# Last feed-forward of a two-block transformer: eight of its eleven up groups by 26 block products instead of 28, the weights' row and column sums on VectorE

## The reference, cut to what matters

```python
def swiglu(y, w_in, w_out):
    a, b = jnp.split(y @ w_in, 2, axis=-1)
    return (jax.nn.silu(a) * b) @ w_out

x = ada_out(x, swiglu(ada_in(x, mod, 2, norm_pre[l, 2]), ffn_w_in[l, 1], ffn_w_out[l, 1]),
            mod, 2, norm_post[l, 2], 0.5)
```

## Time and profile before

| what | value |
|---|---|
| median of 3 runs | 2141.54 us (2141.37 to 2142.06) |
| span of the profiled execution | 2137.4 us |
| TensorE busy | 2103.9 us, 98% of the span |
| VectorE busy | 1093.4 us, 51% |
| GpSimd busy | 721.6 us, 34% |
| ScalarE busy | 514.0 us, 24% |
| TensorE clock granted, mean | 0.997 |

### The profile page before, as it was taken

One profiled execution on the slowest core, in us unless ns is written; L12 is line 12 of the kernel. 1 busy time (PEld: TensorE's weight loads), 2 busy tenths in 40 slices (PEclk: granted clock), 3 DMA queues, 4 the chain that ended last, 5 costly groups with the idle time before them and its releaser, 6 DMA issues. The chain is left out here.

```text
span 2137.4 us, 25867 instructions
## 1 busy us (share of the span) xinstructions
PE 2103.9 (98%) x9961; PEld 1695.4 (79%) x9961; DVE 1093.4 (51%) x2049; ACT 514.0 (24%) x1240; POOL 721.6 (34%) x571
## 2 busy tenths in 40 slices
PE   7999999999999999999999999999999999999998
PEld 4446777777788888888888888888556888888887
DVE  7987956655443873445435534543726341122444
ACT  3443433334440000101400111113234330110101
POOL 0100200000105666654365665630011125456642
PEclk9999999999999999999999999999999999999999
DMA  9752455454222455234135533331222222222231
GB/s 379 238 186 87 137 198 185 141 157 129 81 79 80 158 173 169 55 82 125 48 119 180 174 106 82 82 106 50 77 86 94 65 79 79 79 96 78 75 88 40
DMA packets 244492, 252.27 MB, mean 118 GB/s; under 512 B 9946, under 2 KB 194708, under 8 KB 244116
## 3 DMA queue, kind: packets, MB, share of 16 engines
q1 hardware_dynamic: 243488, 249.17, 36.7%
q10 hardware_dynamic: 884, 1.46, 0.3%
HBM read 245.12 MB, written 4.21 MB: 117 GB/s over the span
## 5 line engine op out<-in xcount | busy, mean ns | idle before, releaser
L2428 POOL TENSOR_TENSOR w_sums<-ring 128x512 f32<-128x512 f32 x66 | 89.3, 1354 | 368.1 <-POOLq L1628 288.3
L2456 POOL TENSOR_TENSOR hidden<-rstd,h_act 128x256 f32<-128x256 f32 x66 | 53.8, 816 | 336.2 <-DVE h_act L2645 336.2
L2645 DVE TENSOR_TENSOR h_act<-ps,rstd 128x256 f32<-128x256 f32 x78 | 33.1, 424 | 221.1 <-PE ps L2328 124.6
L2310 PE MATMUL ps<-h_sums,w_sums 128*128 128x256 f32 x528 | 126.5, 380 | 0.8 <-DVE h_sums L2580 0.4
L2322 PE MATMUL ps<-h_sums,w_sums 128*128 128x256 f32 x528 | 125.0, 379 | 2.0 <-DVE rstd L2614 2.0
L2267 PE MATMUL ps<-h_act,ring 128*128 128x256 f32 x528 | 125.2, 381 | 1.2 <-ACT h_act L1995 1.2
L2333 PE MATMUL ps<-h_act,w_sums 128*128 128x256 f32 x528 | 124.8, 379 | 0.0
L2316 PE MATMUL ps<-h_act,ring 128*128 128x256 f32 x528 | 124.7, 379 | 0.0
L2328 PE MATMUL ps<-h_sums,ring 128*128 128x256 f32 x528 | 124.7, 379 | 0.0
L2275 PE MATMUL ps<-h_act,ring 128*128 128x256 f32 x528 | 124.4, 379 | 0.0
L2614 DVE TENSOR_TENSOR rstd<-ps,h_act 128x256 f32<-128x256 f32 x72 | 30.6, 425 | 164.6 <-PE ps L2310 142.9
(11 more groups left out here) (498 smaller groups left out, 4305.7 us busy)
## 6 DMA issues: line engine op xcount, KB each, us to landing
ring<-in_ffn_w_in SPq DMA_DIRECT2D x66, 1024.0 KB, 7.6
ring<-in_w_mod SPq DMA_DIRECT2D x12, 2048.0 KB, 7.9
ring<-in_w_gate_up SPq DMA_DIRECT2D x22, 1024.0 KB, 7.8
ring<-in_ffn_w_out SPq DMA_DIRECT2D x32, 704.0 KB, 5.7
mod_half<-in_w_ada SPq DMA_DIRECT2D x16, 1024.0 KB, 8.9
ring<-in_w_in SPq DMA_DIRECT2D x7, 2048.0 KB, 10.2
ring<-in_ffn_w_out SPq DMA_DIRECT2D x8, 1408.0 KB, 7.0
ring<-in_w_down SPq DMA_DIRECT2D x16, 704.0 KB, 5.8
```

What stands on the lines that cost most here:

```text
L2310: last = pe.matmul(pb, s2[:, k], F.t2[:, k], start=(k == 0), stop=(k == 3))
L2428: pool.tensor_tensor(s1, a21, a22, ALU.add).then_inc(S["wsum"].sem, 1)
L2456: pool.tensor_tensor(one[:, j], F.gate1[f % 2], F.got21[f % 2], ALU.mult)
L2645: dve.tensor_tensor(out21, pc, F.v, ALU.add).then_inc(S["got21"].sem, 1)
```

## The change

Units 0 to 3 (groups 0 and 1) and units 20 and 21 (group 10) stay as they are. Groups 2 to 9 are each computed as one product of 4x4x2 blocks: the weights' 1024 rows in four blocks of 256, the 512 columns in four blocks of 128, the tokens in two halves. The plain way has 32 block products; this one 26, each of two `matmul` calls, so 52 calls a group. `PAIR_UNITS[2]` names the groups; calls 0 and 1 have none and keep their instructions.

Before the pair groups VectorE forms the token arguments once (`pair_args`: 30 sums of 128x512, both sources in SBUF, drawn by the `spare(2)` of units 0 to 2). For each group TensorE does three rounds of four products with unchanged weights, three rounds of two products with weight differences, four with the row sums and four with the column sums of the weights. GpSimd forms the six differences (128x256 each) and multiplies the hidden values in 128x512 pieces; ScalarE copies 5 pieces out of PSUM and does two silus of 128x512; VectorE forms the rest, and the two sums of the weights, each one `tensor_reduce` over all 4096 elements of a partition. The diff, cut to its core (`F.units` for `UNITS`, `F.ups` for `FT` and the renaming of `f` to `u` are left out):

```diff
+PAIR_UNITS = {0: (), 1: (), 2: tuple(range(2, 10))}
+ROUNDS = (((1, 0), (3, 2)), ((0, 2), (1, 3)), ((0, 3), (1, 2)))
...
+def pair_tensor(K, F, pe, e):
...
+    products(0)
+    if e:
+        R["f"].wait(pe, 3 * e)
+    products(1)
+    R["begun"].wait(pe, 2 * e + 1)
+    differences(0)
...
+        R["full"].wait(pe, e)
+    products(2)
+    R["f"].wait(pe, 3 * e + 1)
+    differences(1)
+    R["w"].wait(pe, 3 * e + 1)
+    R["rows"].wait(pe, e + 1)
+    for i in range(4):
+        last = product(F.round_banks(e, 0)[i // 2], i % 2, F.rows[:, :, i], F.x_val[i], True, i % 2 == 0)
+    last.then_inc(R["d1"].sem, 1)
+    R["f"].wait(pe, 3 * e + 2)
+    differences(2)
+    R["w"].wait(pe, 3 * e + 2)
+    R["cols"].wait(pe, e + 1)
+    for i in range(4):
+        last = product(F.round_banks(e, 1)[i // 2], i % 2, F.cols[:, 2 * i:2 * i + 2], F.block(i, 1), True, i % 2 == 0)
+    last.then_inc(R["d2"].sem, 1)
...
+def pair_rows(K, F, dve, e):
...
+    dve.tensor_reduce(F.rows.rearrange("p k i n -> p (k i n)"), w.rearrange("p (q m) -> p m q", q=4), AX.X,
+                      ALU.add).then_inc(R["rows"].sem, 1)
...
+def pair_vector(K, F, dve, e):
...
+    R["begun"].wait(dve, 2 * e + 2)
+    R["s"].wait(dve, 3 * e + 1)
+    dve.tensor_tensor(w[:, 0:4:3], halves(F.round_banks(e, 0)[0]), total[:, 0:3:2], ALU.subtract).then_inc(R["w"].sem, 1)
+    for r in (1, 2):
...
+        R["y_kept"].wait(dve, 2 * e + r)
+        dve.tensor_tensor(total[:, 0:2], total[:, 0:2], halves(one), ALU.subtract)
+        dve.tensor_tensor(total[:, 2:4], total[:, 2:4], halves(two), ALU.add).then_inc(R["f"].sem, 1)
+    pair_columns(K, F, dve, e)
+    R["s"].wait(dve, 3 * e + 2)
+    dve.scalar_tensor_tensor(w[:, 1:3], halves(F.round_banks(e, 1)[0]), 0.5, yk[0], ALU.mult,
+                             ALU.subtract).then_inc(R["w"].sem, 1)
+    R["w"].wait(dve, 3 * e + 2)
+    dve.tensor_tensor(c[:, 1:3], w[:, 0:2], w[:, 2:4], ALU.add)
+    dve.tensor_tensor(c[:, 0:4:3], w[:, 1:3], w[:, 0:4:3], ALU.subtract).then_inc(R["c"].sem, 1)
+    if last:
+        t2, t1, t4, t3 = F.token_sums(LEAD)
+        dve.tensor_tensor(t3, F.h22, F.h12, ALU.subtract).then_inc(R["token"].sem, 1)
+        R["token"].wait(dve, 1)
+        dve.tensor_tensor(t2, t3, F.h11, ALU.add).then_inc(R["token"].sem, 1)
+    R["d1"].wait(dve, e + 1)
+    R["f"].wait(dve, 3 * e + 2)
+    for i, bank in enumerate(F.round_banks(e, 0)):
+        ins = dve.tensor_tensor(total[:, 2 * i:2 * i + 2], total[:, 2 * i:2 * i + 2], halves(bank), ALU.add)
+    ins.then_inc(R["f"].sem, 1)
+    R["s"].wait(dve, 3 * e + 3)
+    R["c"].wait(dve, 2 * e + 1)
+    dve.tensor_tensor(w[:, 0:2], halves(F.round_banks(e, 2)[0]), yk[1], ALU.subtract).then_inc(R["w"].sem, 1)
...
+    if last:
+        dve.tensor_tensor(t4, F.h21, t2, ALU.subtract).then_inc(R["token"].sem, 1)
+    else:
+        pair_rows(K, F, dve, e + 1)
...
+def pair_differences(K, F, pool, e, r):
...
+        R["s"].wait(pool, 3 * e - 2 + r)
...
+def pair_columns(K, F, dve, e):
...
+    dve.tensor_reduce(F.cols, w.rearrange("p (k i n) -> p k n i", k=KT, i=4), AX.X, ALU.add).then_inc(R["cols"].sem, 1)
...
@@ fast_tensor
+    for u, f in enumerate(F.tiles):
+        if u == LEAD:
+            for e in range(len(F.pairs)):
+                pair_tensor(K, F, pe, e)
...
+            if F.pairs:
+                F.rows_kept.wait(pe, len(ROWS_AT))
+                F.R["w"].wait(pe, 3 * len(F.pairs))
@@ fast_vector
+    if F.pairs:
+        steps = pair_args(K, F, dve)
...
+        if F.pairs and u == LEAD:
+            F.R["hid"].wait(dve, len(F.pairs))
...
+        if F.pairs and LEAD <= u < F.ups:
+            if u > LEAD:
+                S["hid"].wait(dve, u)
+            a, b = (0, 9) if u == LEAD else (9, FH - 1)
+            dve.tensor_tensor(xs[:, a:b], b12[:, a:b], b11[:, a:b], ALU.add).then_inc(S["xsum"].sem, b - a)
@@ kernel
-    nc = bacc.Bacc("TRN2", target_bir_lowering=False, num_devices=1)
+    nc = bacc.Bacc("TRN2", target_bir_lowering=False, num_devices=1, dynamic_dma_scratch_size=1024)
```

More of the change, by code:

```diff
@@ L2196, in fast_fields @@
     F.call, F.prev, F.W, F.context = call, prev, W, context
-    F.S = {n: Tally(K.fast[n], K.fast_base[n]) for n in FAST_COUNTS}
-    for n, count in FAST_COUNTS.items():
+    F.S = {n: Tally(K.fast[n], K.fast_base[n]) for n in FAST_SEMS}
+    F.pairs = PAIR_UNITS[call]
+    F.tiles = [f for f in range(FT) if f // 2 not in F.pairs]
+    F.ups = len(F.tiles)
+    F.units = F.ups + 4
+    for n, count in fast_counts(F.ups).items():
         K.fast_base[n] += count
@@ new lines, in pair_hidden, with pair_weights, product, products @@
+def pair_hidden(F, e, half):
+    f = 2 * F.pairs[e]
+    tiles = F.W.hid[:, :, :, :].rearrange("p a f n -> p (a f) n")
+    a, b = (2 * FH * (f // FH) + FH * half + f % FH for f in (f, f + 1))
+    return tiles[:, a:b + 1:b - a, :]
+def pair_weights(w):
+    return w.rearrange("p (k i n) -> p k i n", k=KT, i=4)
+def pair_tensor(K, F, pe, e):
+    R, S = F.R, F.S
+    w = pair_weights(K.ring.take(pe, ("up", F.call, F.pairs[e])))
+    def product(bank, at, weights, tokens, first, begins):
+        for k in range(2):
+            last = pe.matmul(bank[:, HALF * at:HALF * at + HALF], weights[:, k], tokens[:, k], start=(begins and k == 0),
+                             stop=(k == 1), skip_group_check=True)
+        return last
+    def products(r):
+        one, two = F.round_banks(e, r)
+        for at, (i, j) in enumerate(ROUNDS[r]):
+            R["args"].wait(pe, 2 * r + at + 1)
+            product(one, at, w[:, 2 * j:2 * j + 2, i], F.x_arg[i, j], True, at == 0)
+        for at, (i, j) in enumerate(ROUNDS[r][::-1] if r == 2 else ROUNDS[r]):
+            last = product(two, at, w[:, 2 * i:2 * i + 2, j], F.y_arg[i, j], True, at == 0)
+        last.then_inc(R["t"].sem, 1)
+    def differences(r):
+        one = F.round_banks(e, r)[0]
+        R["diff"].wait(pe, 3 * e + r + 1)
+        for at, (i, j) in enumerate(ROUNDS[r]):
+            last = product(one, at, F.diff[:, r, at], F.s_arg[i, j], False, False)
+        last.then_inc(R["s"].sem, 1)
+    if e == 0:
+        S["got21"].wait(pe, LEAD - 1)
+        S["got12"].wait(pe, LEAD - 1)
+    else:
+        R["w"].wait(pe, 3 * e)
+    products(0)
[4 more added lines that the diff above has]
+    differences(0)
+    if e == 0:
+        S["got21"].wait(pe, LEAD)
+        S["got12"].wait(pe, LEAD)
+    else:
+        R["full"].wait(pe, e)
[14 more added lines that the diff above has]
+    last.then_inc(R["d2"].sem, 1)
+    K.ring.left(R["d2"].sem, R["d2"].base + e + 1)
@@ L2323, in fast_tensor @@
         last.then_inc(S["p5"].sem, 1)
-        if f >= LEAD - 1:
-            sum_11(f)
-        S["w"].wait(pe, f + 1)
+        if u >= LEAD - 1:
+            sum_11(u)
+        S["w"].wait(pe, u + 1)
+        if F.pairs and u == LEAD:
+            F.R["token"].wait(pe, 4)
         for k in range(4):
-            last = pe.matmul(pc, a22[:, k], F.t4[:, k], start=False, stop=(k == 3), skip_group_check=True)
+            last = pe.matmul(pc, a22[:, k], t4[:, k], start=False, stop=(k == 3), skip_group_check=True)
@@ L2560, in fast_scalar @@
         x_square(K, T, act, 0)
[L2561 removed]
+    S["got12"].wait(act, F.units)
     y_square(K, T, act, 9, K.h[:, 3, CTX + HALF:TOK])
```

431 lines of the change are left out of this document (321 added, 110 removed).

## The result

The changed kernel takes 2180.39 us (median of 4 runs, 2179.04 to 2180.70) against 2141.45 us before: 1.0183 times the time, 95% interval 1.0171 to 1.0196. The prediction was 2168 us, range 2139 to 2198. So the sign and the range held, and the number was 12 us short.

A forecast was written before the change was run, and what follows sets the result against it. TensorE bounds the kernel before; in the pair groups its loop through w3 and VectorE's own work were to meet at 26.0 us. Pair groups +14.7, arguments +8.4 and leaving the pairs +3.5 gave +26.6 us: 2168 us, range 2139 to 2198.

The forecast's parts named there:

- Price of the reductions: In `pair_rows` and `pair_columns`, each VectorE reduction over 4096 elements takes 7.4 us, the middle between 4.4 and 10.5.
- the upper end: 10.5 us for each reduction, at 2.54 ns an element, from the hopping write of L1154.
- VectorE's other work: VectorE's operations in a pair group beside the two reductions take 11.0 us, waits included.
- The cycle: Pair group: TensorE's loop through w2 and w3 and VectorE's own work both 25.8 us; 26.0 a group, +14.7 for eight.
- t3: The end of `products(2)` of a pair group, taken as time zero; unhindered, the next comes 22.45 us later.
- Two signs: In the pair groups: TensorE idle before `products(0)`, released by VectorE; VectorE's share in the steady stretch near 100%.
- dear reductions: Rival, pair groups: reductions cost nearer to the hopping write, R = 10.5 us; 2180 to 2216 us, 2195 its number; chance 0.22.
- Arguments: Units 0 to 2: VectorE's 30 argument sums put 8.4 us on the path, p5 waiting for v; from nothing to 11.
- Leaving the pairs: Last group and unit 20: p1 waits 2.4 us for w3, p5 another 1.1 to 1.8; together 3.5, from 2 to 5.
- GpSimd, ScalarE, SyncE at nothing: Pair groups: GpSimd some 8 us of 26, ScalarE below 5, SyncE's loads unchanged; none adds time.
- The contiguous reductions: Rival, pair groups: reductions run at the in-order price, R = 4.4 us; 23.6 a group, 2149 us (2138 to 2158); chance 0.30.
- The faster case: Rival: contiguous reductions, hidden arguments (`spare` pair below 1.39 us), no contention at the c sums; 2136 us; chance 0.10.

## Why the prediction was right or wrong

- **Price of the reductions: right, by luck.** 7.4 us was taken as the middle between in order and a hopping write; 7.35 and 7.23 were measured, and in order 4.4, the lower end. But the write that gave the upper end was not slow by its hop alone. GpSimd was busy beside it, and VectorE's sums just ahead of it, which hop nowhere, took 1.21 us for the usual 0.69 (kernel before, VectorE, then GpSimd):

```profile
77.08 1.21 DVE L1148 TENSOR_TENSOR raw_t<-raw_t,cst 128x512 f32<-128x512 f32 x1
78.21 1.21 DVE L1150 TENSOR_TENSOR tmp<-tmp,cst 128x512 f32<-128x512 f32 x1
79.45 1.46 DVE L1154 TENSOR_TENSOR kv_t<-raw_t,tmp 128x512 f32<-128x512 f32 x1
...
75.66 9.13 POOL L1119 TENSOR_TENSOR h_act<-x_res,ctx_rstd 128x256 f32<-128x256 f32 x8 [24.33 <-ACT ctx_rstd L1100]
```

  Against these neighbours the hopping write costs 0.25 us more, not 0.77. By that the upper end would have been 6.2 us and the middle 5.3 (estimates); how the hop and GpSimd's work add up no run shows. So that the write agrees with a page's price for small hops says little. The Trainium skill's 1.73 ns an element (Vector Engine (DVE) Microarchitecture Reference, section 5.2) is close to the 1.77 and 1.79 measured; its remark on a single stream that alternates between two regions at full rate doesn't carry over to these two reads.
- **VectorE's other work: right.** The PSUM sums take 0.68 to 0.69 us, the 256-wide ones 0.42; a steady group's eighteen instructions beside the reductions keep VectorE busy for 10.4 us, where 11.0 were forecast with the waits.
- **The cycle: right as far as it went.** w2 10.4 us behind t3 was the forecast; 1822.39 + 10.08 = 1832.47 is where the column products start. 26.0 us a group were forecast, 25.8 are measured where the clock stays up. Two signs did not come. The gap ahead of `products(0)` is none: by the forecast's own numbers the column products end at 10.4 + 3.45 = 13.9, behind w3 at 13.6. And VectorE was busy for 24.95 of the second group's 27.41 us, 91% and not near 100%: the loop through w2 sets the pace, not VectorE's total, as the run with the rows in order shows.
- **The step that failed** is in "The cycle of a pair group": TensorE's products behind a wait were priced at 0.432 us a call, the price of an engine that never idles. Behind the waits they ran at half clock, which cost 16.5 us in the groups and 1.75 in unit 20. This term was missing, and it alone is more than the 12 us by which the forecast was short. The loop itself, at full clock, is 25.6 us (10.08 + 3.45 + 12.09) and not 26.0, which takes 3 us off again. That the time still lies in the range is luck: its upper part stood for dear reductions, and these were not dear. The forecast named the wait of 3 us and did not ask what it does to the clock. The Trainium skill has the rule (TensorE: Matmul & The Clock Gate, "Part 1: The HAM clock gate"): the array's clock falls to 1.2 GHz behind idle time. The granted clock of 0.50 behind the gap agrees.
- **Arguments: right in size.** 8.4 us forecast, 7.6 measured, with waits for w, v and got22 where only v was named. The slack of v is 0.99 us by its rows, not 1.1.
- **Leaving the pairs: right for w3, hidden for p5.** 2.4 us were forecast ahead of p1, 2.2 are measured. The 1.1 us ahead of p5 did not show: v is there at 2013.26, and p5 starts at 2014.04, 1.75 us late already by the slow products. At full clock it would have come to 2012.29 and waited about 1.0 us (an estimate); in the run with the rows in order, where unit 20's products are not slow, p5 waits 0.80 us.
- **GpSimd, ScalarE, SyncE at nothing: right** in the changed kernel; no gap of TensorE in this stage names them. The comparison "against 11.6 x 2 before" is misread: GpSimd's 107.38 us of the earlier trace rows over sixteen units are 6.7 a unit, 13.4 a group.
- **Small slips.** 26.0 less 24.18, eight times, is 14.6 and not 14.7. Half-way to the dear reductions is +50, 2192 us and not 2195. That each call shows as two instructions is seen in every trace; that float32 is the reason, as said ahead, no run here shows.
- **The rivals.** The contiguous reductions were put at 2149 us, 23.6 a group; the two runs with the columns in order gave 2147 and 2152, and 23.7 in the latter. The faster case was ruled out rightly on both its conditions: the `spare` pairs of units 0 to 2 took 1.9 us in the mean, above its 1.39, and the collision at the c sums is real, 1.1 us (0.8 forecast).

## What to carry to other kernels

Saving products on a saturated TensorE moved the bound here to the engine that forms the sums. Write out the chain from one product to the next that depends on it, not only each engine's total. Of two equal savings of 2.9 us on VectorE, one gave 33 us, slow products included, and the other 1 (one run each); and the place of an operation counted too (22.5 against 23.7 us a group for the same adds). A reduction over a hopping view was dearer than adds over long runs of the same data: three adds of 1024 took 3.7 us, and 5.4 beside GpSimd's work, one reduction of 4096 took 7.3. Before a row serves as a price, look at what the other engines did at its time.

## What the runs showed that was not expected

- **Idle time costs twice.** Behind a 3.0 us gap, eight calls took 5.1 to 6.7 us for 3.6, up to as much again as the gap. Gaps of 0.8 to 1.5 us in units 1 to 3 left the next eight instructions at 1.97 to 1.99 us, with a granted clock of 1.00. It is not the same each time: behind 3.12 us unit 20's p5 took 1.99 us in one version, behind 3.13 us 3.50 in the next.
- **A faster engine gained nothing.** With both reductions cheap, VectorE and GpSimd fell into step at the c sums in every group. The steady groups took as long as with one dear reduction, and the exit 3 us longer.
- **Reductions beside GpSimd.** Each of the two reductions of the changed kernel varies by 0.1 us at most (7.28 to 7.38 and 7.22 to 7.24), while GpSimd's sums ran beside them. VectorE's sums with two sources in SBUF grew beside GpSimd's, from 0.69 to 1.25 us for 128x512 in the version with both in order; those with a source in PSUM kept their 0.68.
